# The neighbours of a rotary embedding: eight float32 products, or small transfers within SBUF on ScalarE's queue

## What is computed

```python
def rope_partial(t, cos, sin):
    half = ROPE_DIM // 2                    # 8
    ...
    t1 = t[..., :half]
    t2 = t[..., half:ROPE_DIM]
    return jnp.concatenate([t1 * c - t2 * s, t2 * c + t1 * s, t[..., ROPE_DIM:]], axis=-1)

def second_block(...):
        h = rmsnorm_2(x, norm1_g[l])
        proj = jnp.einsum('bsd,de->bse', h, w_in[l])
        dq, dk, dv, fq, fk, fv, fg = jnp.split(proj, SPLITS, axis=-1)
        dq = rope_partial(dq.reshape(B, S, DIFF_HEADS, 2, DIFF_DH), cos, sin)
        dk = rope_partial(dk.reshape(B, S, DIFF_HEADS, 2, DIFF_DH), cos, sin)
        ...
```

## Time and profile before

| | |
|---|---|
| median of 3 runs | 1866.41 us (1864.88 to 1867.08) |
| profiled execution | 1864.9 us, its span 1862.8 us |
| granted TensorE clock, mean | 0.996 of full speed |
| PE busy | 1835.7 us, 99% of the span |
| VectorE, ScalarE, GpSimd busy | 919.4, 739.9, 279.2 us (49, 40, 15%) |
| chain that ended last | PE 88%, DVE 6%, ACT 4%, DMA 1%, issue 1% |

### The profile page before, as it was taken

The page is one execution under the profiler, slowest core; times in us unless marked ns, Lnnn a source line. Parts: engine busy times, 40 slices in busy tenths (PEclk is TensorE's granted clock), DMA queues, the critical chain, the costliest instruction groups (busy, mean ns, idle before and its releaser), DMA issues.

```text
span 1862.8 us, 21743 instructions
## 1 busy us (share of the span) xinstructions
PE 1835.7 (99%) x8924; PEld 1495.7 (80%) x8924; DVE 919.4 (49%) x1449; ACT 739.9 (40%) x1179; POOL 279.2 (15%) x246
## 2 busy tenths in 40 slices
PE   9999999999999999999999999999999999999998
PEld 7777788888888887778888888877876788888886
DVE  6666555543454456535543344456666433323334
ACT  5645344332332446644432233342556332222223
POOL 2001222220121200002321022112001122201210
PEclk9999999999999999999999999999999999999999
DMA  6122122322222332213223222221121222322321
GB/s 237 46 97 74 68 91 91 105 99 91 90 96 91 130 134 78 84 46 114 91 91 107 97 91 85 96 102 69 68 102 42 84 91 95 109 91 90 107 80 62
DMA packets 31810, 172.91 MB, mean 93 GB/s; under 512 B 3792, under 2 KB 5968, under 8 KB 13792
## 3 DMA queue, kind: packets, MB, share of 16 engines
q1 hardware_dynamic: 26320, 162.02, 24.3%
q10 hardware_dynamic: 5392, 9.51, 1.6%
HBM read 169.38 MB, written 2.13 MB: 92 GB/s over the span
## 4 chain that ended last, share of the span: by engine, by line
PE 88%; DVE 6%; ACT 4%; DMA 1%; issue 1%; POOL 0%; SPq 0%; DVEq 0%; ACTq 0%; POOLq 0%
PE ps L966 50%; PE ps L1223 19%; PE ps L894 6%; PE ps L985 5%; PE ps L1127 2%; PE ps L1082 2%; DVE WL L1701 1%; PE ps L1107 1%; PE ps L1166 1%; DMA raw<-in_wall 1%; PE ps L1147 1%; ACT WH L1295 1%; ACT PB L1453 1%; PE ps L874 1%; DVE k L1840 0%
## 5 line engine op out<-in xcount | busy, mean ns | idle before, releaser
L966 PE MATMUL ps<-hH,WH 128*128 128x512 f32 x1456 | 574.2, 394 | 3.1 <-DVE O L1799 1.8
L966 PE MATMUL ps<-hH,WL 128*128 128x512 f32 x1456 | 567.5, 390 | 0.0
L966 PE MATMUL ps<-hL,WH 128*128 128x512 f32 x1456 | 567.4, 390 | 0.0
L1701 DVE TENSOR_TENSOR WL<-raw,WH 128x1024 fp32r<-128x1024 f32 (+2 forms) x308 | 380.4, 1275 | 362.3 <-ACT WH L1295 362.1
L1295 ACT ACTIVATE WH<-raw 128x1024 fp32r<-128x1024 f32 (+2 forms) x308 | 301.6, 1027 | 295.4 <-PE ps L1223 228.6
L966 PEld LDWEIGHTS ps<-hH,WH 128*128 128x128 f32 x1456 | 273.6, 188 | 68.0 <-issue 7.9
L966 PEld LDWEIGHTS ps<-hL,WH 128*128 128x128 f32 x1456 | 273.8, 188 | 58.0 <-issue 2.2
L966 PEld LDWEIGHTS ps<-hH,WL 128*128 128x128 f32 x1456 | 273.7, 188 | 57.6
L1223 PE MATMUL ps<-fH,WH 128*128 128x512 f32 x528 | 205.4, 389 | 0.0
L1223 PE MATMUL ps<-fL,WH 128*128 128x512 f32 x528 | 205.4, 389 | 0.0
L1223 PE MATMUL ps<-fH,WL 128*128 128x512 f32 x528 | 205.4, 389 | 0.0
(11 more groups left out here) (345 smaller groups left out, 1996.4 us busy)
## 6 DMA issues: line engine op xcount, KB each, us to landing
raw<-in_wall SPq DMA_DIRECT2D x140, 1024.0 KB, 4.6
raw<-in_wall SPq DMA_DIRECT2D x12, 768.0 KB, 4.0
bias<-in_bias ACTq DMA_DIRECT2D x12, 256.0 KB, 3.0
X<-in_xt SPq DMA_DIRECT2D x8, 256.0 KB, 8.6
CB<-rows ACTq DMA_DIRECT2D x8, 256.0 KB, 3.5
out_y<-X SPq DMA_DIRECT2D x3, 512.0 KB, 3.0
raw<-in_wall SPq DMA_DIRECT2D x4, 256.0 KB, 5.6
mrA<-in_memt ACTq DMA_DIRECT2D x4, 256.0 KB, 6.1
```

The lines of the kernel that those rows point to most:

```text
L966: mm = e.matmul(ps[b][:, 0:N], ww[:, k, c:c + 128], x[:, k, 0:N], start=(k == 0 and i == 0), stop=(k == 7 and i == 2))
L1701: e.tensor_tensor(WL[n % NCV][:, c], raw[n % NRAW][:, c], WH[n % NCV][:, c].bitcast(F32), ALU.subtract).then_inc(*mark("wl", n, x))
```

## The change

The eight products with `rotm` go, and with them `rotm` itself, a block of the constants. A step `rope` is added to ScalarE's list, at the place of the tile's sink: it waits for `U1` of the tile, and then issues four transfers within SBUF, of 8 rows x 512 float32 (16 KB) each, from `U1` to the neighbours' rows in `U2`: rows 8 to 15 to rows 0 to 7 and back, and the same from row 64. The signs are now in the table of sines. VectorE waits for the four landings in place of the product, and multiplies `U2` by `RS` within SBUF (L2097 before, L2099 of the changed kernel). GpSimd sets both `U2` to zero once, in the step `chunk_bias`, well before the first tile. Its semaphores for tiles set once are put together in one, `set`, which changes no order. The last filler products (`keep`) take `ident` in place of `rotm`.

```diff
+                elif what == "rope":
+
+                    name, m = a
+                    w.wait_ge(*at("ropeU", name, m))
+                    w.wait_ge(*at("set", "U0"))
+                    for x in ROPE_BEFORE[(name, m)]:
+                        w.wait_ge(*at(*x))
+                    for r in (0, 8, 64, 72):
+                        o = r + 8 if r % 64 == 0 else r - 8
+                        e.dma_start(U2[m % 2][r:r + 8, :], U1[m % 2][o:o + 8, :]).then_inc(s_U[m % 2], 16)
...
-                elif what == "rope_later":
-                    name, m = a
-                    b, before = bank(("rope", name, m), ("ropeR", name, m))
-                    if before:
-                        w.wait_ge(*at(*before))
-                    w.wait_ge(*at("ropeU", name, m))
-                    e.matmul(ps[b][:, :], rotm, U1[m % 2][:, :], start=True, stop=True).then_inc(
-                        *mark("roped", name, m))
...
                 elif what == "rope_later":
                     name, m = a
                     dst = dq if name == "dq" else dk
-                    w.wait_ge(*at("roped", name, m))
+                    w.wait_ge(s_U[m % 2] if ev.sems else None, 64 * (ROPE_SEQ.index((name, m)) // 2 + 1))
+                    w.wait_ge(*at("set", "U0"))
                     w.wait_ge(s_RS if ev.sems else None, 16)
-                    for x in ROPE_BEFORE[(name, m)][2:]:
-                        w.wait_ge(*at(*x))
-                    e.tensor_tensor(U2[m % 2][:, :], ps[BANK[("rope", name, m)]][:, :], RS[:, :], ALU.mult).then_inc(
+                    e.tensor_tensor(U2[m % 2][:, :], U2[m % 2][:, :], RS[:, :], ALU.mult).then_inc(
                         *mark("ropeR", name, m))
...
+                e.memset(U2[0][:, :], 0.0).then_inc(*mark("set", "U0h"))
+                e.memset(U2[1][:, :], 0.0).then_inc(*mark("set", "U0"))
...
-        S[b:b + 8] = np.sin(ang)
+        S[b:b + 8] = np.sin(ang) if b % 64 else -np.sin(ang)
```

More of the change, by code:

```diff
@@ L617, in program @@
         cols = place("cols", [128, NCOLS])
-        K = place("K", [128, 5, 128])
+        K = place("K", [128, 4, 128])
         KB = place("KB", [128, 3, 128], BF16)
@@ L725, in program @@
         identb, mchunk, mcaus = (KB[:, i, :] for i in range(3))
-        ident, ones, rotm = (K[:, i, :] for i in (0, 1, 4))
+        ident, ones = (K[:, i, :] for i in (0, 1))
         gz, gt, ga, gm, gE = (O[0:4, i, :] for i in range(1, 6))
@@ L739, in program @@
         s_CB = [sem(f"CB{i}") for i in range(2)]
+        s_U = [sem(f"U{i}") for i in range(2)]
         s_rows = sem("rows")
@@ L901, in tensor @@
                     b, _ = bank("start", None)
-                    w.wait_ge(*at("zero"))
+                    w.wait_ge(*at("set", "zero"))
                     for i in range(8):
@@ L934, in tensor @@
                     w.wait_ge(*at("gwD", a[0]))
-                    w.wait_ge(*at("gw0"))
+                    w.wait_ge(*at("set", "gw0"))
                     for k in range(8):
@@ L947, in tensor @@
                     for i in range(a[0]):
-                        mm = e.matmul(ps[b][:, 0:128], ones, rotm, start=True, stop=True)
+                        mm = e.matmul(ps[b][:, 0:128], ones, ident, start=True, stop=True)
                     mm.then_inc(*mark("kept"))
@@ L1156, in tensor @@
                     w.wait_ge(*at("mtri", hd, JL[-1][0]))
-                    w.wait_ge(*at("vones"))
+                    w.wait_ge(*at("set", "vones"))
                     for t0 in (0, 2):
@@ L1857, in vector @@
                         if u["kind"] == "diff":
-                            w.wait_ge(*at("chunk"))
+                            w.wait_ge(*at("set", "chunk"))
                         if u["kind"] == "fox":
@@ L2158, in gpsimd @@
                 if what == "start":
-                    e.memset(diag[:, :], 0.0).then_inc(*mark("zero"))
-                    e.memset(gw[:, :, :], 0.0).then_inc(*mark("gw0"))
+                    e.memset(diag[:, :], 0.0).then_inc(*mark("set", "zero"))
+                    e.memset(gw[:, :, :], 0.0).then_inc(*mark("set", "gw0"))
                     e.memset(small[:, 60:61], 1e-6).then_inc(*mark("eps", 0))
@@ L2166, in gpsimd @@
                     for n, (c, size) in enumerate(V_ONES):
-                        e.memset(vA[:, :, c:c + size], 1.0).then_inc(*(mark("vones") if n else mark("vonesh")))
+                        e.memset(vA[:, :, c:c + size], 1.0).then_inc(*(mark("set", "vones") if n else mark("set", "vonesh")))
                 elif what == "fence":
@@ L2303, in sync @@
             e.dma_start(cols[:, :], colsd).then_inc(s_cols, 16)
-            e.dma_start(K[:, :, :], consts.rearrange("p (i c) -> p i c", i=5)).then_inc(s_K, 16)
+            e.dma_start(K[:, :, :], consts.rearrange("p (i c) -> p i c", i=4)).then_inc(s_K, 16)
             e.dma_start(gsum[:, :], gatew[:, 64:72]).then_inc(s_gw, 16)
@@ L2344, in program @@
         ROPE_SEQ = [(n, m) for n in ("dq", "dk") for m in range(4)]
-        ROPE_BEFORE = {x: ([] if i < 2 else [("roped",) + ROPE_SEQ[i - 2], ("ropeC",) + ROPE_SEQ[i - 2],
-                                             ("rope",) + ROPE_SEQ[i - 2]]) for i, x in enumerate(ROPE_SEQ)}
+        ROPE_BEFORE = {x: ([] if i < 2 else [("ropeC",) + ROPE_SEQ[i - 2], ("rope",) + ROPE_SEQ[i - 2]])
+                       for i, x in enumerate(ROPE_SEQ)}
         OD_BEFORE = {0: [("accP", "n1", 6), ("acc2", 7)], 1: [("accP", "n1", 7), ("acc2", 6)], 2: [("odsum", 0)],
@@ L2404, in shape_constants @@
     causal = np.where(i[None, :] <= i[:, None], np.float32(0), np.float32(NEG)).astype(np.float32)
[L2405 to L2410, removed]
+    consts = np.concatenate([ident, ones, chunk, causal], 1)
     inv = np.float32(500000.0) ** (-np.arange(0, 16, 2, dtype=np.float32) / np.float32(16))
```

4 lines of the change are left out of this document (2 added, 2 removed).

## The result

| | before | after |
|---|---|---|
| median of 21 runs each | 1866.06 us (1864.43 to 1867.44) | 1869.18 us (1867.21 to 1871.74) |
| ratio, 95% interval | | 1.0018 (1.0012 to 1.0024) |
| profiled execution, its span | 1864.9, 1862.8 us | 1870.09, 1868.3 us |

The change makes the kernel 3.1 us slower. The forecast was 1861.1 with a range up to 1867.0, so the time lies outside it, and the sign is wrong: the interval leaves out no change, though by 0.18% only.

A forecast was written before the change was run, and what follows sets the result against it. TensorE, busy for 99% of the span, was taken as the bound. Dropping products gives 8.7 us, less 0.35 waiting at `dv` is 8.35, of which bank waits at the third scores leave 5.3: 1866.4 - 5.3 = 1861.1 us, range 1857.2 to 1867.

The forecast's parts named there:

- I take 0.40, between them: ScalarE's queue: pitch of transfer issues taken as 0.40 us, between rows of 0.30 and 0.46.
- VectorE's time at the scores: Attention's start, where VectorE takes the scores out: 3.5 us earlier than before, at 1307.1 against 1310.64.
- issues of dq 0 and dq 1, up to ScalarE's exponential: Rotation's first pair: ScalarE issues until 1253.95, and the forget gate's exponential starts at 1258.05 in place of 1260.39.
- `U1` to `U2`: Issue and landing of a tile's four transfers: 2.9 us for dq, 3.5 us for dk beside a weight load.
- ScalarE held ahead of a weight unit: ScalarE's list at dq 3, dk 1 and dk 3: four issues hold it 1.6 us each, 4.8 together.
- A change in exposed or held comes out of the gain one for one: Changes in four exposed transfers (12.8 us) or three holds (4.8) reduce the gain equally, up to 8.7.
- The products: TensorE's rotation products go: 8.7 us together, the gain if nothing comes late.
- in time by 1.2 at dk 2, late by 0.35 at dv: TensorE's wants for `WL`: first unit ready 1.2 us early at dk 2, second a new 0.35 us wait at `dv`.
- the gain of 2.3 at `U1` of dq 2: VectorE and ScalarE chain behind the forget gate moves up 2.3 us: `U1` of dq 2 ready at 1268.15, not 1270.44.
- the third scores: TensorE waits there for fk 0's bank: 1.4 us of room, so at most 5.3 us of its 8.35 stay.
- Just made up for: Rival: pitch 0.46 and landing 2.6 cancel the gain through waits for weights and banks; 1864.9 us, chance 0.32.
- The slower one: Rival: exposed transfers stand behind the weight loads, 6.4 us each, a loss of 7.5; 1873.9 us, chance 0.07.

The follow-up runs named there:

- experiment 8: Changed kernel plus eight groups of probe transfers on ScalarE's queue in the last feed-forward part; own time not of interest, issues within SBUF 0.60 to 0.63 us.
- experiment 5: Changed kernel with two of each tile's four transfers issued from SyncE's queue, two from ScalarE's; 1862.86 us, ratio to before 0.9979.
- experiment 2: Changed kernel with one of the four transfers per tile, three left out; 1857.85 us, ratio to before 0.9950.
- experiment 9: Changed kernel with 14 thrown-away products filling TensorE's idle time ahead of dk 2's first product; 1869.18 us, ratio to before 1.0014.

## Why the prediction was wrong

**What stopped it: the pitch of the issues.** The step "I take 0.40, between them" rests on two rows, both of issues with HBM at one end (0.30, and 0.46 for 128 rows). No row of before had both ends in SBUF. It measured 0.68, outside both ends of the range that I gave it. The sum went on by VectorE's time at the scores: forecast 3.5 us earlier, measured 4.8 later, a gap of 8.3. By the prediction's own steps, each measured against its value:

| step | forecast | measured | cost |
|---|---|---|---|
| issues of dq 0 and dq 1, up to ScalarE's exponential | 1258.05 | 1262.40 - 1.99 | 2.4 |
| `U1` to `U2` at dq 2 | 2.9 | 4.0 | 1.1 |
| the same at dk 0 and dk 2 | 3.5 each | 4.3, 4.2 | 1.5 |
| ScalarE held ahead of a weight unit, three times | 1.6 each | 2.7 each | 3.3 |

Together 8.3: the gap to the tenth. Nearly all of it is the issues' price, eight of them in series in the first row; the rest is the landing, 2.0 (experiment 8) where I took 1.7 for dq. At dk 0 and dk 2 it is 2.0 as well (1288.9 to 1290.90 at dk 0), less than the 2.3 that I took, but one issue of each four takes 0.9 there.

**The rule was right.** "A change in exposed or held comes out of the gain one for one": 5.3 - 8.3 = -3.0, which from 1866.4 makes 1869.4; measured 1869.18. The prediction had put that at 1:1 and then tried pitches from 0.30 to 0.46 only. From its own numbers the point where the gain is gone lay at a pitch of about 0.59: four exposed transfers with three issues each ahead of the last, three holds of four, and one more set of four where dq 0 and dq 1 are issued in series, 28 issues, so 5.3 / 28 = 0.19 above 0.40. The 28 issues at 0.68 make 7.8 of the 8.3. That last set was missing from the rule as I wrote it: the pair dq 0, dq 1 was one exposed transfer of the four.

**The products.** Their 8.7 us stand: without transfers 8.8 us came back between the two places (10.3 by the medians).

**The waits.** Forecast in time by 1.2 at dk 2, late by 0.35 at dv: `WL` came 4.6 later than in the sum (2.4 + 1.1 + 1.1) and TensorE waited 3.39 and 1.87. The forget gate's product was forecast at 1255.2 and started at 1257.30 - 1.99 = 1255.31, and TensorE's wait of 1.43 at dq 2 was gone. The claim that the gain of 2.3 at `U1` of dq 2 would come did not hold: it is ready at 1272.43 - 1.99 = 1270.44, to the hundredth the time of before.

**The bank.** I let only the third scores be late, with 1.4 us of room for fk 0's way out. The first place that bound was fq 0's, for the bank of fk 0's product: before, fq 0 was out at 1322.5 and the product started at 1325.17, a room of 2.65. VectorE came 4.6 later, and TensorE's product 2.0 later. But the place that I had bound too, and bound last: VectorE took out fk 0 4.1 later (1342.78 - 1.99 against 1336.67), and the third scores, stopped at the bank that it held, took 1.3 us longer than before. The view shows 0.38 of that as a wait. TensorE left them 3.27 late, where the sum gives 3.0.

**The rivals.** "Just made up for" had the right picture with too small a pitch, 0.46, and too long a landing, 2.6; it ended 4.3 us short of the measured time. The slower one was for the wrong reason: the transfers do not stand behind the weight load. At dk 0 and dk 2, with a load under way, `U1` to `U2` took 4.3 and 4.2, at dq 2 without one 4.0; so 0.2 to 0.3 us is the price of the load, where the forecast had 0.6 and that rival 3.5. The trace shows it as one longer issue, 0.89 at dk 0 and 0.87 at dk 2. The load is over by the fourth transfer (share of the DMA engines 0.98 up to 1288.5 and 0.40 in the half microsecond behind, fourth issue at 1288.9); with two issues in a row (experiment 5) it is not, and the difference was 0.4 to 0.9. What was missing is a rival with the pitch of a kind of issue that no row showed. The Trainium skill, DMA: Bandwidth & Descriptors, section Issuing engines are not separate DMA queues, says that issuing from several engines saves only the time of the sequencer, "which is usually small relative to the DMA itself". Here that time was 2.7 of the 4.0 us between `U1` and `U2`, and a second issuing engine saved 0.9 of them at dq 2 (experiment 5): for small transfers within SBUF the trace does not bear out the "usually small".

**Port.** `WL` took 2.36 in the changed kernel, as in the sum: the lateness kept it away from GpSimd. Where it came back on time it took 3.45, which is part of why undoing the hold gave 6 to 7 us and not the 8.1 of three holds.

**The clock** was not in the forecast. It fell, and the filling of the wait showed that this costs nothing while VectorE leads.

## What to carry to other kernels

Count a transfer by three prices: its issue on the queue (times all that are issued in a row, also for what stands behind them on that engine), its landing, and the place where its reader waits. When one engine's small work is replaced by transfers, look first for the order in which the reader can do its next tile meanwhile; here that was worth 11.7 us (1869.18 to 1857.45), with the transfers as slow as before. A price that no row of the profile shows needs a range wider than its nearest rows, and the forecast should name the value at which the sign turns.

## What was not expected of the hardware

- An issue within SBUF takes 0.60 to 0.63 us on its engine (0.74 to 0.89 for single ones beside a weight load; pitch 0.68 for eight in a row), against 0.31 with HBM at one end, whatever the rows (4 to 32) and bytes (64 B to 2 KB a row) within SBUF; on ScalarE's queue and on SyncE's alike (0.63 and 0.62).
- A small transfer within SBUF is visible to the waiting engine 2.0 us after the start of its issue when it is the last of four, and 2.3 when it is alone (experiment 8); alone, it is 2.7 us behind the `U1` that it waits for (experiment 2).
- TensorE's clock fell to 0.50 behind idle times of 3.39 and 2.42 us, for some 3.5 us each, and behind one of 3.05 (experiment 9) for 6.8; behind idle times of 1.87 and 2.83 us in the changed kernel it read 1.00. Behind one and the same wait of 2.6 us, that for `diag`, it fell in eight traces, before among them, and read 1.00 in four, after among them. What decides is not shown.
